# A two-layer decoder with routed experts on one core: the router by halves of the tokens, and the first expert matrix's gather by chunks

## The chip, the cores and the metric

One Trainium2 (trn2) chip, of which one core is used. The metric is the device time of one execution in microseconds; the time before is the median of three executions. All arithmetic is in float32.

## The reference, cut to what matters

Two layers over 256 tokens of width 1024. In each layer a mixer is added to x (retention and a gated linear recurrence in layer 0, stick-breaking and differential attention in layer 1), and then a mixture of experts:

```python
x = x + mix
h = rms_norm(x, norm_ffn[l])
g_logits = h @ wg_r + bg_r                 # 4 groups: the best one is taken
e_logits = h @ we_r + be_r                 # 32 experts, 8 in a group: the best two of the group
gate = p_g * softmax(top_v)                # p_g: the group's softmax probability
a = silu(xb @ w_gate[e]) * (xb @ w_up[e])  # per expert, 1024 -> 512
y = a @ w_down[e]                          # 512 -> 1024, weighted by gate and summed per token
x = x + y
```

rms_norm divides each token's row by the root of its mean square and multiplies by a gain per column. Each expert's three matrices hold 2 MiB each; all 32 experts of both layers are read, 402 MB of the 447 MB that the kernel moves.

## The kernel before

The kernel gives each engine a program of its own, tied by semaphores (`then_inc`, `wait_ge`). Names end in the layer; "half" below means 128 of the 256 tokens (`tc` 0 or 1), which are the partitions of one tile.

**Weights.** SBUF has twelve places of 2 MiB (`places`). The sync engine's program issues every load in a fixed order (lines 436 to 498). Before each it waits until TensorE's count `unit_used` says that the place is free. A unit is one expert's matrix; experts go in quads of four, with twelve units (four of `w_gate`, four of `w_up`, four of `w_down`). When the router begins, the units of quad 0 are loaded or under way; the thirteenth (u = 12) goes into the place of the first. In the gate matrix of quad 0 the four units are stored by quarters of the rows (`QUARTERED`): TensorE frees one after each two chunks of 128 rows. Units 12 to 15 are loaded one by one, those from 16 on four at a time (`load_matrices`, line 391), when all four of a matrix are free. The up matrix of quad 0 is what load 16 waits for.

**The end of the mixer.** `project_out` (line 1109) makes the sums of the output projection. VectorE adds them to x: half 0 whole, half 1 in two parts of 512 columns (lines 1545 to 1551). TensorE transposes x (`turn_x`), and ScalarE copies it into hT and takes the squares (`finish_mixer`, line 1364). The norm's roots are asked for by VectorE (`norm_root`, `inverse_root`), begun by ScalarE with a logarithm and an exponential (`take_root`, line 861), and refined by VectorE with four narrow steps (lines 856 to 859). `ROOTS` lists the requests in order; both engines follow it.

**The router.** TensorE, in this order (`route_and_experts`, line 1140): the strips of half 0 (the router's weights by hT, eight matmuls), a transposition, the first four strips of half 1, the logits of half 0, the other strips of half 1, `start_sums` for accumulator bank 0 (x by the identity, which puts x into the sums of the experts' outputs), the logits of half 1 once ScalarE has copied its strips, `start_sums` for banks 1 to 3, and two filler matmuls (`keep_busy`). VectorE (`route`, line 1582) waits for the logits of both halves, scales them by the roots and adds the bias (line 1602), and finds for each expert by how many of its group it is beaten: differences of all pairs (line 1605), a comparison (1606), a sum (1608), 640 elements wide each; then the group mask (1609) and `picked` (1611). TensorE counts by matmuls with a triangle of ones at which place in its expert each token stands (lines 1170 to 1174), and VectorE keeps it in `rank` (1617).

**The gather.** Each expert has 32 slots in a pass, a quad 128. `one_hots` (line 796) builds `sel`, tokens by slots, by comparing `rank` with 1 to 32 (793), and multiplies it by the roots (799). TensorE multiplies x by it, chunk by chunk of 128 columns, both halves summed in PSUM (line 577); ScalarE writes each chunk to xT with the gain (line 743). For quad 0 TensorE gathers chunks 0 to 3, multiplies chunks 0 and 1 by the gate matrix (line 631), gathers 4 to 7, and goes on. Then, for this and every other quad: up matrix; gather for the next quad; silu(gate) times up by ScalarE and VectorE (lines 760, 820, 823); transpositions (673, 675) of it and of the weighted one-hots `selw`; down matrix; and the outputs are spread back to the tokens (line 565) while the next gate matrix runs. The combine weights are made in `gates` (line 1627) behind the one-hots, with two exponentials on ScalarE (`route`, line 1378) and a load of the sigmoid table behind them. `largest_count` gives the largest number of tokens of an expert; with more than 32, further passes follow (`pe.If(count > SLOTS)`).

## Time and profile before

| | |
|---|---|
| median of three executions | 1168.0 us (1166.81 to 1169.35) |
| the profiled execution's own time | 1166.55 us |
| its span, first to last instruction | 1164.8 us |
| TensorE matmuls busy | 876.4 us (75%) |
| VectorE, ScalarE busy | 223.8 us (19%), 126.7 us (11%) |
| moved by DMA | 447.45 MB, mean 384 GB/s |
| mean granted TensorE clock | 0.877 of full |

The profile is one execution with a record for each instruction. Lines (L631) are lines of the kernel before. An instruction's busy time says what it took, the chain of waits says which work the end of the run hung on, and a table of stretches says what each engine and the DMA engines did between two moments. A float32 matmul appears as two records (x16 is eight matmuls).

### The profile page before, as it was taken

To read this page: it belongs to the slowest core of one execution; us is meant where nothing else is said; L and a number is where in the kernel's file an instruction comes from. 1 tells how busy PE (TensorE), PEld (TensorE's weight loads), DVE (VectorE), ACT (ScalarE), POOL (GpSimd) and SP (SyncE) were. 2 spreads that over 40 slices of the span, in tenths; PEclk is the share of its full clock that TensorE was granted. 3 is DMA by queue.
4 is the path that set the end of the run, shared out by engine and by line. 5 is a ranking of instruction groups with operands and counts; after the bars stand their busy time and mean duration, and the time that the engine had idled before them with its cause. 6 is when DMAs were issued, how large, how long until landed. Compare 5 with 4: busy or idle time off the path is not lost.

```text
span 1164.8 us, 11459 instructions
## 1 busy us (share of the span) xinstructions
PE 876.4 (75%) x5104; PEld 394.0 (34%) x5104; DVE 223.8 (19%) x470; ACT 126.7 (11%) x249; POOL 0.5 (0%) x5
## 2 busy tenths in 40 slices
PE   8999999747474738485899999977474747474776
PEld 7555554212121212121246655433131313131312
DVE  2732332010101010101127541410000101000001
ACT  3411311000000000000021431200000000000000
POOL 0000000000000000000000000000000000000000
PEclk9999999888888877777999999998787878788889
DMA  9776659999999999999996477899999999999997
GB/s 347 304 321 257 267 219 378 430 435 433 435 433 433 435 433 435 435 430 414 424 423 284 154 293 276 317 441 433 433 435 435 433 435 433 433 430 432 417 426 308
DMA packets 19637, 447.45 MB, mean 384 GB/s; under 512 B 2560, under 2 KB 2816, under 8 KB 5504
## 3 DMA queue, kind: packets, MB, share of 16 engines
q1 hardware_dynamic: 19584, 446.67, 91.0%
q8 instruction: 43, 0.70, 0.2%
q14 instruction: 10, 0.08, 0.0%
HBM read 445.61 MB, written 1.05 MB: 383 GB/s over the span
## 4 chain that ended last, share of the span: by engine, by line
DMA 56%; PE 42%; DVE 1%; another core or an unknown queue 1%; issue 0%; ACT 0%; SPq 0%; DVEq 0%
DMA places<-in_together 47%; PE psum L631 14%; PE psum L1016 11%; DMA places<-in_quarters 8%; PE psum L1117 5%; PE psum L1013 4%; PE psum L577 1%; PE psum L1029 1%; PE psum L1057 1%; PE psum L565 1%; DMA places<-in_w_in 0%; PE psum L1144 0%; PE psum L698 0%; PE psum L968 0%
## 5 line engine op out<-in xcount | busy, mean ns | idle before, releaser
L631 PE MATMUL psum<-places,mixed 128*32 128x512 f32 x3040 | 421.8, 707 | 276.3 <-DMA places<-in_together 249.2
L631 PEld LDWEIGHTS psum<-places,mixed 128*32 128x32 f32 x3040 | 110.4, 127 | 570.5 <-issue 448.7
L1016 PE MATMUL psum<-places 128*128 128x512 f32 x288 | 126.3, 593 | 0.0
L1016 PEld LDWEIGHTS psum<-places 128*128 128x128 f32 x288 | 53.6, 190 | 61.4 <-issue 61.2
L577 PEld LDWEIGHTS psum<-sel,x 128*128 128x128 f32 x528 | 60.4, 192 | 17.0 <-issue 15.1
L577 PE MATMUL psum<-sel,x 128*128 128x128 f32 x528 | 64.3, 279 | 1.7 <-DVE sel L799 1.7
L565 PE MATMUL psum<-y_sb,spread 128*128 128x512 f32 x128 | 59.6, 606 | 2.1 <-ACT y_sb L768 1.4
L820 DVE TENSOR_TENSOR sig<-psum,sig 128x512 f32<-128x512 f32 x16 | 11.1, 692 | 253.4 <-ACT sig L760 253.4
L823 DVE TENSOR_TENSOR mixed<-psum,sig 128x512 f32<-128x512 f32 x16 | 11.1, 692 | 245.4 <-PE psum L631 245.4
L833 DVE COPY y_sb<-psum 128x512 f32<-128x512 f32 x14 | 9.7, 692 | 180.2 <-PE psum L631 180.2
L762 ACT COPY mixed<-psum 128x512 f32<-128x512 f32 x16 | 9.4, 586 | 320.6 <-PE psum L675 320.6
L1013 PE MATMUL psum<-places 128*128 128x256 f32 x192 | 42.9, 381 | 0.0
L1013 PEld LDWEIGHTS psum<-places 128*128 128x128 f32 x192 | 36.1, 190 | 5.7 <-issue 1.0
L760 ACT ACTIVATE sig<-psum 128x512 f32<-128x512 f32 x16 | 9.6, 597 | 255.9 <-PE psum L631 255.9
L565 PEld LDWEIGHTS psum<-y_sb,spread 128*128 128x128 f32 x128 | 22.8, 189 | 38.6 <-issue 33.7
L768 ACT COPY y_sb<-psum 128x512 f32<-128x512 f32 x16 | 9.4, 586 | 209.2 <-PE psum L631 181.8
L1117 PE MATMUL psum<-places,y_sb 128*128 128x512 f32 x64 | 28.2, 594 | 0.7 <-ACT small L1396 0.7
L1117 PE MATMUL psum<-places 128*128 128x512 f32 x64 | 28.5, 592 | 0.0
L826 DVE TENSOR_TENSOR mixed<-psum,consts 128x512 f32<-128x512 f32 x32 | 21.9, 690 | 31.8 <-PE psum L577 31.8
L1117 PEld LDWEIGHTS psum<-places,y_sb 128*128 128x128 f32 x64 | 11.9, 190 | 14.8 <-issue 13.9
L1388 ACT ACTIVATE places<-psum,small 128x512 f32<-128x512 f32 x16 | 10.1, 684 | 57.7 <-PE psum L1016 53.6
L1117 PEld LDWEIGHTS psum<-places 128*128 128x128 f32 x64 | 11.8, 190 | 13.4 <-issue 13.4
(252 smaller groups left out, 505.4 us busy)
## 6 DMA issues: line engine op xcount, KB each, us to landing
places<-in_singles SPq DMA_DIRECT2D x32, 2048.0 KB, 10.1
places<-in_quarters SPq DMA_DIRECT2D x22, 2048.0 KB, 35.1
places<-in_w_in SPq DMA_DIRECT2D x12, 2048.0 KB, 26.7
places<-in_w_out SPq DMA_DIRECT2D x4, 2048.0 KB, 14.3
places<-in_quarters SPq DMA_DIRECT2D x4, 1024.0 KB, 45.6
places<-in_w_in SPq DMA_DIRECT2D x2, 1024.0 KB, 27.2
places<-in_w_in SPq DMA_DIRECT2D x3, 512.0 KB, 8.7
x<-in_x SPq DMA_DIRECT2D x2, 512.0 KB, 13.6
```

Source lines behind the costliest of these rows:

```text
L565: mm = pe.matmul(psum[:, ACC + 2 * n + tc, :], spread[:, tc, :], y_sb[:, 512 * n:512 * (n + 1)], start=False, stop=False, skip_group_check ...
L577: mm = pe.matmul(psum[:, YB + c // 4 if bank is None else bank, (c % 4) * P:(c % 4 + 1) * P], x[:, tc, c * P:(c + 1) * P], sel[:, tc, :], ...
L631: mm = pe.matmul(psum[slots, out + n, :], inp[:, c, slots], slot(layer, unit)[:, at + 512 * n:at + 512 * (n + 1)], start=c == 0, stop=c == ...
L820: turn(nc.vector.tensor_tensor(sig, psum[:, GATE, :], sig, ALU.mult))
L823: nc.vector.tensor_tensor(flat(act_h), psum[:, UP, :], sig, ALU.mult).then_inc(m["act_ready"], 1)
L826: nc.vector.tensor_tensor(xT[:, 4 * half:4 * half + 4, :], psum[:, 6 + half, :].rearrange("p (c s) -> p c s", s=P), gain_cols[:, 2 + layer ...
L1013: mm = pe.matmul(banks[:, m // 2, (m % 2) * SEQ:(m % 2 + 1) * SEQ], w[:, c, m * P:(m + 1) * P], hT[:, c, :], start=c == 0, stop=c == KC - 1)
L1016: mm = pe.matmul(banks[:, m, :], hT[:, c, m * P:(m + 1) * P], w[:, c, :], start=c == 0, stop=c == KC - 1)
L1029: mm = pe.matmul(psum[:, 4 + m, 0:SEQ], w[:, c, m * P:(m + 1) * P], hT[:, c, :], start=c == 0, stop=c == KC - 1)
L1057: mm = pe.matmul(banks[:, m, :], hT[:, c, m * P:(m + 1) * P], w[:, c, :], start=c == 0, stop=c == KC - 1)
L1117: return pe.matmul(psum[:, OUT_BANK[layer] + 2 * tc + n, :], mixT(half)[:, c, tc * P:(tc + 1) * P], w[:, c, 512 * n:512 * (n + 1)], start= ...
L1388: r = nc.scalar.activation(dst[:, tc * 512:(tc + 1) * 512], proj(g)[:, tc, :], function, scale=small[:, 2 + tc:3 + tc])
```

## The change

- **Roots by half.** Each layer asks for two roots, one per half. Half 0's is asked for as soon as its square is there, while the output matmuls of half 1 run; half 1's behind the picks of half 0. ScalarE serves the second one ahead of its copy of half 1's strips.
- **Router by half.** Scores, differences, comparison, sum, mask and pick are done for half 0 (320 wide) once its logits are there, then for half 1. Ranks are one matmul for half 0, and two in one sum for half 1. The last addition to x moves from the end of the mixer to the head of `route`, in the same place of VectorE's order. The best expert's mask moves to `gates`.
- **No roots in the one-hots.** `sel` stays 0 or 1. Two matmuls of one column (`scale_slots`) bring the roots of the tokens to their slots, ScalarE keeps them in `slot_scale`, and they enter in the sigmoid's scale and in VectorE's two products.
- **Gather by chunks.** For quad 0, half 0's share of chunks 0 and 1 is gathered when half 0's one-hots are there, then half 1's, then the scale; chunks 2 and 3 are gathered ahead of the third chunk of the gate matrix, 4 and 5 ahead of the fourth, 6 and 7 ahead of the sixth. The exponentials and the table load of ScalarE follow the last of these.
- **TensorE's order.** `start_sums` for bank 0 stands between the ranks of half 0 and of half 1, and for banks 1 to 3 between the gate and the up matrix of quad 0; the counting of the largest number is a pair of matmuls behind the gather of chunks 2 and 3; the count is read ahead of the last quad's branch.

```diff
...
-ROOTS = ((2, 2), (20, 8), (28, 8), (2, 2), (2, 2), (44, 16), (44, 16), (44, 8), (2, 2))
+ROOTS = ((2, 2), (20, 8), (28, 8), (2, 1), (3, 1), (2, 2), (44, 16), (44, 16), (44, 8), (2, 1), (3, 1))
...
+def count_picked(pe):
+    pe.matmul(psum[:, 5, 64:96], ones[:, 0:P], picked[:, 0, :], start=True, stop=False)
+    pe.matmul(psum[:, 5, 64:96], ones[:, 0:P], picked[:, 1, :], start=False, stop=True).then_inc(S["ranks_done"], 1)
...
+    def scale_slots(bank):
+        for tc in range(TC):
+            mm = pe.matmul(psum[:, bank, SEQ:SEQ + 1], sel[:, tc, :], small[:, 2 + tc:3 + tc], start=tc == 0, stop=tc == TC - 1)
...
-    def gather_rest():
-        gather_chunks(4, 8).then_inc(m["gathered"], 1)
-        pe.wait_ge(m["xT_ready"], 1)
+            gather_some(4 * half, 4 * half + chunks, YB + half, range(TC)).then_inc(m["gathered"], 1)
+    def begin_gather():
+        pe.wait_ge(S["sel_first"], layer + 1)
+        gather_some(0, 1, YB + 1, (0,))
+        gather_some(1, 2, YB, (0,))
+        pe.wait_ge(m["sel_ready"], 1)
+        gather_some(0, 1, YB + 1, (1,)).then_inc(S["gather_begun"], 1)
+        gather_some(1, 2, YB, (1,))
+        scale_slots(YB).then_inc(S["gather_begun"], 1)
+    def go_on_gathering(c):
+        begun = 3 * layer
+        if c == 0:
+            pe.wait_ge(S["xT_begun"], begun + 1)
+        elif c == 1:
+            pe.wait_ge(S["xT_begun"], begun + 2)
+        elif c == 2:
+            gather_some(2, 4, YB + 1, range(TC)).then_inc(m["gathered"], 1)
+            count_picked(pe)
+            pe.wait_ge(m["xT_ready"], 1)
+        elif c == 3:
+            gather_some(4, 6, YB, range(TC)).then_inc(S["gather_begun"], 1)
+        elif c == 4:
+            pe.wait_ge(S["xT_begun"], begun + 3)
+        elif c == 5:
+            gather_some(6, 8, YB + 1, range(TC)).then_inc(m["gathered"], 1)
+        elif c == 6:
+            pe.wait_ge(m["xT_ready"], 2)
...
+            matrix(0, 0, GATE, xT, KC, FF, each_chunk=go_on_gathering)
+            start_sums(pe, layer, (1, 2, 3))
+            pe.wait_ge(S["route_ready"], layer + 1)
...
-        mm.then_inc(m["turned"], 1)
+            pe.transpose(psum[:, UP, tc * P:(tc + 1) * P], selw[:, tc, :], ident)
+        scale_slots(UP).then_inc(m["turned"], 1)
...
+    count = pe.value_load(over_i[0:1, layer:layer + 1], min_val=0, max_val=SEQ)
     with pe.If(count > SLOTS):
...
+    def begin_gathered():
+        begun = 3 * layer
+        act.wait_ge(S["gather_begun"], begun + 1)
+        gained_chunks(0, 1, YB + 1, 0).then_inc(S["xT_begun"], 1)
+        act.wait_ge(S["gather_begun"], begun + 2)
+        gained_chunks(1, 2, YB, 0).then_inc(S["xT_begun"], 1)
+        keep_scale(YB)
+        act.wait_ge(m["gathered"], 1)
+        gained_chunks(2, 4, YB + 1, 0).then_inc(m["xT_ready"], 1)
+        act.wait_ge(S["gather_begun"], begun + 3)
+        gained_chunks(4, 6, YB, 0).then_inc(S["xT_begun"], 1)
+        act.wait_ge(m["gathered"], 2)
+        gained_chunks(6, 8, YB + 1, 0).then_inc(m["xT_ready"], 1)
+        gate_exps(layer)
...
-        nc.scalar.activation(sig, psum[:, GATE, :], ACT.Sigmoid).then_inc(m["sig_ready"], 1)
+        nc.scalar.activation(sig, psum[:, GATE, :], ACT.Sigmoid, scale=slot_scale).then_inc(m["sig_ready"], 1)
         act.wait_ge(m["turned"], n16 + i + 1)
         nc.scalar.copy(actT, psum[:, GATE, :].rearrange("p (c s) -> p c s", c=FC))
+        keep_scale(UP)
...
-        placed(sel, quad)
-        nc.vector.tensor_tensor(sel, sel, small[:, 2:4].unsqueeze(2).broadcast_to([P, TC, P]),
-                                ALU.mult).then_inc(m["sel_ready"], 1)
+        placed(sel, quad).then_inc(m["sel_ready"], 1)
...
-        nc.vector.tensor_tensor(flat(act_h), psum[:, UP, :], sig, ALU.mult).then_inc(m["act_ready"], 1)
+        nc.vector.scalar_tensor_tensor(flat(act_h), psum[:, UP, :], slot_scale, sig, ALU.mult, ALU.mult).then_inc(m["act_ready"], 1)
...
+def mean_square(dve, layer, tc):
+    dve.wait_ge(S["squares"], SQUARES[2 * layer] + (1, 3)[tc])
+    return nc.vector.tensor_scalar(small[:, 2 + tc:3 + tc], small[:, tc:tc + 1], 1.0 / D, EPS, ALU.mult, ALU.add)
...
-        logits(0)
+        logits(0).then_inc(S["logits_done"], 1)
         pe.wait_ge(S["xT_third"], layer + 1)
-        strips(1, range(KC // 2, KC)).then_inc(S["strips"], 1)
-        start_sums(pe, layer, (0,))
+        strips(layer, 1, range(KC // 2, KC)).then_inc(S["strips"], 1)
         pe.wait_ge(S["last_strips_kept"], layer + 1)
         logits(1).then_inc(S["logits_done"], 1)
-        start_sums(pe, layer, (1, 2, 3)).then_inc(S["sums_started"], 1)
+        pe.wait_ge(S["picked_ready"], TC * layer + 1)
+        pe.matmul(psum[:, 4, 0:32], before, picked[:, 0, :], start=True, stop=True).then_inc(S["ranks_done"], 1)
+        start_sums(pe, layer, (0,))
+        pe.wait_ge(S["scores_read"], layer + 1)
+        pe.matmul(psum[:, 5, 0:32], ones[:, 0:P], picked[:, 0, :], start=True, stop=False)
         keep_busy(pe, 2, 7, ident, consts[:, 0:SEQ])
-        pe.wait_ge(S["picked_ready"], layer + 1)
-        both = picked.rearrange("p c e -> p (c e)")
-        pe.matmul(psum[:, 5, 0:64], before, both, start=True, stop=False, skip_group_check=True)
-        mm = pe.matmul(psum[:, 5, 32:64], ones[:, 0:P], picked[:, 0, :], start=False, stop=True, skip_group_check=True)
-        mm.then_inc(S["ranks_done"], 1)
-        pe.matmul(psum[:, 4, 0:32], ones[:, 0:P], picked[:, 0, :], start=True, stop=False)
...
+        pe.wait_ge(S["picked_ready"], TC * layer + 2)
+        pe.matmul(psum[:, 5, 0:32], before, picked[:, 1, :], start=False, stop=True).then_inc(S["ranks_done"], 1)
         moe_pe(pe, layer, 0, 0)
...
         keep_xT(layer, 0, slice(0, 2), nc.scalar.copy).then_inc(S["xT_first"], 1)
+        take_root(act, turn)
...
+        ask_root(mean_square(dve, layer, 0), 2, 1)
         dve.wait_ge(S["out_second"], layer + 1)
         V.tensor_tensor(x[:, 1, 0:512], x[:, 1, 0:512], sums(1)[:, 0:512], ALU.add).then_inc(S["added"], 1)
+        refine_root(dve, turn)
...
+        def differences(tc):
+            turn(V.tensor_tensor(by_duel(tc), rows_of(tc).unsqueeze(2).broadcast_to(each),
+                                 rows_of(tc).unsqueeze(3).broadcast_to(each), ALU.subtract))
+        def pick(tc):
+            by_row = pairs(tc).rearrange("p (r n) -> p r n", r=n_rows)
+            turn(V.tensor_tensor(by_row, by_row, const("earlier_wins").unsqueeze(1).broadcast_to([P, n_rows, PER_GROUP ** 2]),
+                                 ALU.is_gt))
+            turn(V.tensor_reduce(beaten_by[:, tc].rearrange("p (r e) -> p r e", e=PER_GROUP), by_duel(tc), AX, ALU.add))
+            turn(V.tensor_scalar(g_hot[:, tc], beaten_by[:, tc, N_EXPERTS:N_EXPERTS + N_GROUPS], 1.0, None, ALU.is_lt))
+            in_group = g_hot[:, tc].unsqueeze(2).broadcast_to([P, N_GROUPS, PER_GROUP])
+            and_wait(dve, V.scalar_tensor_tensor(by_group(picked[:, tc]), by_group(beaten_by[:, tc, 0:N_EXPERTS]), 2.0, in_group,
+                                                 ALU.is_lt, ALU.mult), S["picked_ready"], TC * layer + tc + 1)
+        def place_first(tc):
+            dve.wait_ge(S["ranks_done"], 3 * layer + tc + 1)
+            turn(V.scalar_tensor_tensor(rank[:, tc, 0:32], psum[:, 4 + tc, 0:32], 1.0, picked[:, tc], ALU.add, ALU.mult))
+            return V.tensor_tensor(sel[:, tc].rearrange("p (e s) -> p e s", e=TILE),
+                                   const("iota").unsqueeze(1).broadcast_to([P, TILE, SLOTS]),
+                                   rank[:, tc, 0:TILE].unsqueeze(2).broadcast_to([P, TILE, SLOTS]), ALU.is_equal)
...
+        finish_x(layer)
+        dve.wait_ge(S["strips"], TC * layer + 1)
+        keep_strips(0, V.tensor_copy).then_inc(S["strips_kept"], 1)
+        dve.wait_ge(S["squares"], SQUARES[2 * layer] + 2)
+        scores(0)
+        differences(0)
+        pick(0)
+        dve.wait_ge(S["squares"], SQUARES[2 * layer + 1])
+        turn(V.tensor_tensor(small[:, 1:2], small[:, 1:2], small[:, 7:8], ALU.add))
+        ask_root(mean_square(dve, layer, 1), 3, 1)
+        refine_root(dve, turn)
+        scores(1)
+        V.memset(small[:, 60:61], 0.0).then_inc(S["scores_read"], 1)
+        differences(1)
+        pick(1)
+        place_first(0).then_inc(S["sel_first"], 1)
+        place_first(1).then_inc(M[layer]["sel_ready"], 1)
+    def largest_count(layer):
+        sc = rt[:, 18:19]
+        dve.wait_ge(S["ranks_done"], 3 * layer + 3)
+        turn(V.tensor_reduce(sc[:, 0:1], psum[:, 5, 64:96], AX, ALU.max))
...
+        largest_count(layer)
         dve.wait_ge(S["group_exp"], layer + 1)
...
```

## Rows read from the trace of the kernel before

**Rows 1.** The page, part 4: the chain that ended last, by engine.
```profile
...
DMA 56%; PE 42%; DVE 1%; another core or an unknown queue 1%; issue 0%; ACT 0%; SPq 0%; DVEq 0%
...
```

**Rows 2.** Stretches: PE, PEld, DVE, ACT, POOL busy (instructions), PEclk, DMA share, GB/s.
```profile
...
176.10:179.00 2.90, 2.90 (x26) 1.34 (x25) 1.46 (x9) 2.27 (x6) 0.00 (x0) 1.00 0.04 11
179.00:199.00 20.00, 19.05 (x175) 9.36 (x177) 5.62 (x12) 2.60 (x7) 0.00 (x0) 1.00 0.99 404
199.00:589.00 390.00, 252.19 (x1694) 90.08 (x1686) 35.13 (x63) 14.30 (x28) 0.00 (x0) 0.82 1.00 432
...
741.30:744.00 2.70, 2.70 (x25) 1.14 (x24) 1.34 (x8) 2.23 (x6) 0.00 (x0) 1.00 0.03 6
...
764.00:1154.00 390.00, 252.53 (x1698) 90.25 (x1690) 35.09 (x63) 14.30 (x28) 0.00 (x0) 0.81 1.00 431
...
```

**Rows 3.** Layer 0's chain from strips to second matrix: start, us, what.
```profile
...
166.75 0.34 PE psum L1149 x2
...
167.69 1.06 PE psum L558 x2
...
169.00 0.44 DVE mixed L1602 x2
...
169.46 0.84 DVE mixed L1605
...
172.52 0.43 PE psum L1170 x2
172.95 0.21 PE psum L1171 x2
...
173.25 0.24 DVE rank L1617
...
173.51 0.44 DVE sel L793
...
173.97 0.43 DVE sel L799
...
174.45 2.05 PE psum L577 x16
176.51 1.85 PE psum L631 x16
178.36 1.98 PE psum L577 x16
180.34 12.28 PE psum L631 x112
...
192.63 28.94 DMA places<-in_together
```

**Rows 4.** VectorE (DVE) in order of time, layer 0's router.
```profile
...
165.63 0.29 DVE L979 COPY mixed<-psum 128x128 f32<-128x128 f32 x1 [0.35 <-PE psum L1144]
...
167.16 0.16 DVE L856 TENSOR_TENSOR small<-small 128x2 f32<-128x2 f32 x1 [0.72 <-ACT small L867]
...
167.75 0.16 DVE L859 TENSOR_TENSOR small<-small 128x2 f32<-128x2 f32 x1
...
```

**Rows 5.** ScalarE (ACT) in order of time, layer 0's router.
```profile
...
166.69 0.21 ACT L866 ACTIVATE small<-small 128x2 f32<-128x2 f32 x1
166.92 0.20 ACT L867 ACTIVATE small<-small 128x2 f32<-128x2 f32 x1
...
175.65 0.63 ACT L743 ACTIVATE mixed<-psum,consts 128x128 f32<-128x128 f32 x2 [7.65 <-PE psum L577]
...
```

**Rows 6.** TensorE (PE) in order of time, layer 0's router.
```profile
...
168.72 2.82 PE L558 MATMUL psum<-x,consts 128*128 128x512 f32 x6
171.38 1.03 PE L553 MATMUL psum<-consts 128*128 128x256 f32 x4
...
```

**Rows 7.** Stretches around one wait of TensorE, columns as in rows 2.
```profile
...
543.60:547.40 3.80, 0.01 (x1) 0.01 (x1) 0.27 (x1) 0.00 (x0) 0.00 (x0) 1.00 1.01 431
...
548.30:552.20 3.90, 0.58 (x1) 0.00 (x0) 0.00 (x0) 0.00 (x0) 0.00 (x0) 0.50 1.01 429
...
```

158 lines of the change are left out of this document (68 added, 90 removed).

## The prediction

> **What bounds the kernel.** I read the page first. Transfers hold 56% of the chain that ended last and TensorE 42% [rows 1]. A share says nothing of what a change in one stage is worth, so the next view is a table of stretches [rows 2]. From 199 us to 589 us in layer 0, and from 764 us to 1154 us in layer 1, the DMA engines are busy all the time, at 432 and 431 GB/s. That is the stream of expert weights. No engine's work in these 780 us shortens the run, unless it keeps the stream from its start. Just ahead of it the engines are empty: 11 GB/s from 176.1 to 179.0 us, 6 GB/s from 741.3 to 744.0 us. All twelve places are full, and the next unit (u = 12) may be fetched only when TensorE has used the first quarter of the first gate matrix. So the price of the router is read there: each microsecond by which that quarter is used earlier moves the whole stream, and all behind it, by one, as long as the stream then has no hole. The waits of the router that don't reach this point are worth nothing.
>
> The chain through layer 0's router is next [rows 3]. The logits of the first half end at 166.75 + 0.34 = 167.09 us. VectorE begins with them only at 169.00, when both halves are there. One-hots with the roots multiplied in are ready at 174.40. TensorE gathers four chunks (2.05 us), multiplies the first two (1.85 us), and frees the quarter at 178.36 us. The third transfer of the stream, which fetches a whole matrix, is issued at 192.63, when the up matrix is used. Layer 1 has the same gap 565 us later [rows 2], and I take its chain as a copy of layer 0's.
>
> **What the change does to the quarter.** I rebuild the chain for layer 0, with 0.03 to 0.04 us between two dependent VectorE steps and 0.06 to 0.11 us from one engine to another, as the starts and ends in rows 3 leave between them.
> - VectorE can begin at 167.09 + 0.11 = 167.20, which is 1.8 us earlier. The strips themselves stand where they stood, and the new root of the first half lies ahead of them, while the output matmuls run; it costs nothing, and without this cover it would cost the 1.2 us that the next root is priced at. On ScalarE it moves the first-half square by about 0.4 us, which nothing waits for.
> - Three passes are done by halves, 320 wide in place of 640. A 640-wide pass takes 0.84 us [rows 3], a 256-wide one 0.44: 1.04 ns an element, so 0.50 us for 320 wide, 0.53 with its gap. Between the nearest rows the bounds are half of 0.84 (0.42) and 0.50; I take 0.50, because 256 wide is near. First half: scores 0.25, three passes 1.59, group mask 0.21, pick 0.20, so picked at 169.45.
> - Then the second half's root stands in the middle: an addition and a mean (0.36 with gaps, by the 0.16 us of a narrow step [rows 4]), ScalarE's logarithm and exponential (166.69 to 167.12 us [rows 5], 0.5 with the hand-over), four refining steps (167.16 to 167.91 us [rows 4], 0.75). It ends near 171.15. Behind this wait ScalarE also holds back the copy of the second half's strips, which it does after the root (0.27 us, 170.4 to 170.7), and TensorE the logits behind that, until 171.1: late by 2.4 us, and just hidden by the refining.
> - Second half: scores and marker 0.31, passes 1.59, mask and pick 0.41: picked at 173.46, which is 1.0 us later than now (172.48, where rows 3 has TensorE start at 172.52). Rank (0.24) and a one-hot of half the width (0.30, as 128 wide takes 0.29 [rows 4]) follow for each half: 174.06 and 174.63. The ranks of the second half are one matmul, 0.43 us [rows 3], ready at 174.0, in time. Saved here: the multiplication by the roots, 0.43. So the one-hots are ready at 174.63 in place of 174.40, 0.23 us later.
> - TensorE: a gather matmul takes 2.05/8 = 0.26 us. The two of the first half (0.51) run before 174.63; the two of the second end at 175.20; two matmuls with the roots follow, 0.21 each (the narrow ones of rows 3): 175.62. ScalarE's first chunk (0.63 us for two [rows 5]) is ready at 175.4. Two chunks of gate, 1.85: the quarter is free at 177.47 in place of 178.36.
>
> **Gain per layer: 0.9 us; with both, 1.8 us**, and the rest is whether the stream stays whole. The second quarter: gather 1.03, counting matmuls 0.42, a stall of 0.35 for ScalarE's two chunks, a chunk of 0.88, gather 1.03, a chunk of 0.88: 182.06 us, as now (178.36 + 1.98 + 1.75). A 2 MiB unit at 432 GB/s takes 4.85 us; begun at about 178.1 it ends at 183.0, when the next is just due. I take off 0.1 us a layer. The third transfer: the sums of banks 1 to 3 now stand between gate and up, 2.7 us [rows 6]. From the quarter to the end of up is 3.09 + 0.42 + 0.35 + 12.28 + 2.7 = 18.8 us, so 196.3 in place of 192.63, 3.7 us later. Four units at 432 GB/s last 19.4 us, to about 198.3. From the issue (178.4) to first data was under 1 us, since 20 us at 404 GB/s are 8.1 of the 8.4 MB [rows 2]. So this edit costs nothing, under a cover of 1 us; with that gone, all beyond is paid.
>
> By the Trainium skill, DMA: Bandwidth & Descriptors, section Latency and other measured facts, a first byte comes some 600 ns after the issue; by this the cover would be 1.4 us and the sum the same. It agrees with rows 2 as a bound.
>
> A rule speaks against the halves: VectorE: DVE Perf Modes, section The TRN2 errata, of the Trainium skill says that each instruction pays a fixed time, so that small tiles pay it more often, and gives (N + 151)/0.96 ns; by this 320 wide is 0.49 us and the sum is unchanged. The 0.84 us of the 640-wide row agrees.
>
> In the quads: one 0.43 us VectorE pass fewer, two narrow matmuls and a ScalarE copy of one column more, all under the stream, where TensorE is busy 252 of 390 us [rows 2]. Cover gone, they would cost 0.6 us in each of 16 quads. The count is read by TensorE just ahead of the last quad, also in a wait.
>
> **Sum:** 2 x 0.8 = 1.6 us off the profiled execution's 1166.55 (span 1164.8), so 1164.95. That execution is 1.45 us under the median of 1168.0; on that scale, 1166.4 us, or 0.14% faster. A measurement of this kernel can tell 0.2%, 2.3 us, from no change.
>
> **The rivals.**
> - *More gain* (chance 0.26). If a halved pass takes near half (0.42), three passes of each half save 0.5 us a layer more, and if hand-overs are on the short side, 0.3 more: 2.4 to 3.2 us in all, 1164.8 to 1165.6. For it: picks and masks are also narrower. Against: the fixed part of the narrow rows.
> - *The clock of TensorE* (0.14), the case on the other side. From 167.7 to 170.7 us TensorE now waits for the held-back strips, where it ran sums before (from 167.69 [rows 3]), and until 174.1 has only some 3 us of work. In this trace the clock went to its lower level (0.50, 1.2 GHz) after a wait of 3.8 us (543.6 to 547.4) with little work behind it [rows 7]. The new wait is 3.0. If it falls there, the sum of bank 0 and the filler (1.03 us [rows 6]) take twice as long and the second half's ranks start at 175.5 in place of 173.5: 2.0 us, less the gain, 1.2 us slower a layer; if it stays low through gather and the first chunks, 2.8 more. In all 2.4 to 8 us slower, 1170.4 to 1176. It decides if the wait is long enough to bring the clock down, in both layers. If in one alone, there is no change. The Trainium skill's page TensorE: Matmul & The Clock Gate, section HAM oscillation, has the same rule, that waits make the clock fall and it must be earned again; rows 7 agree.
> - *The gain is eaten* (0.10). The up matrix ends over 1 us later than I have it, or the second quarter does, and the stream has holes of up to 0.8 us a layer: 1166 to 1168.5. The stream is then no longer moved by the router, but by TensorE's work after it.
>
> **Chances.** The forecast has 0.50. Faster by over 0.2%: the first rival and the edge of the forecast, 0.28. Slower by over 0.2%: most of the clock case, 0.13. Within: 0.59. The range goes from 1164.0, the larger gain with the scatter of a median, to 1170.0, the lower end of the clock case.
>
> **What would show it.** Per layer: picked for the second half about 1.0 us later against the strips; a wait of TensorE of 3 us after the strips; the first gate matmul about 0.8 us earlier; the DMA gap shorter by 0.9 us; the third transfer issued 3.7 us later with no gap in DMA ahead of it. I am wrong if the DMA rate dips near 197 to 199 us, if the granted clock falls in the router, or if the stream's 780 us change in length.

## The result, and the profile after

The changed kernel takes 1172.17 us (median of 6 runs, 1170.87 to 1176.85); the kernel before, beside it, 1168.05 us (6 runs). The ratio is 1.0040, 95% interval [1.0030, 1.0051]: 0.4% slower, where 1166.4 us and a small gain were forecast. The profiled execution took 1170.87 us, with a span of 1169.1 us. Its page has 11669 instructions in place of 11459, and part 4 begins:

```profile
DMA 49%; PE 47%; another core or an unknown queue 1%; issue 1%; ACT 1%; DVE 1%; SPq 0%; DVEq 0%
```

Against [rows 1], 7 points have gone from the transfers to TensorE, ScalarE and "issue". The end no longer hangs on the last weights alone.

The stretches of the changed kernel, with the columns of [rows 2]; the last two are those in which the profile has a low clock:

```profile
176.10:179.00 2.90, 2.90 (x26) 1.45 (x26) 0.19 (x1) 0.58 (x3) 0.00 (x0) 1.00 0.06 17
179.00:199.00 20.00, 19.65 (x154) 8.19 (x153) 4.73 (x17) 4.04 (x10) 0.00 (x0) 1.00 0.98 392
199.00:589.00 390.00, 253.31 (x1764) 96.58 (x1762) 35.36 (x60) 16.31 (x38) 0.00 (x0) 0.83 1.00 431
...
173.40:176.80 3.40, 3.40 (x20) 2.95 (x22) 2.43 (x12) 0.55 (x2) 0.00 (x0) 0.61 0.87 371
736.60:743.40 6.80, 6.68 (x25) 5.29 (x25) 4.32 (x20) 0.27 (x2) 0.00 (x0) 0.55 0.84 355
```

The stream still runs at 431 GB/s, and TensorE's load in it is as before. New is the clock (the column after the engines): 0.61 and 0.55 in the two routers, so mostly at the lower level of 1.2 GHz. TensorE in order of time, layer 0's router (start, us, engine, line, in brackets the wait before it):

```profile
170.74 0.41 PE L1176 MATMUL psum<-both_strips,mixed 128*128 128x40 f32 x2 [2.84 <-ACT mixed L1038]
...
171.20 1.10 PE L559 MATMUL psum<-x,consts 128*128 128x512 f32 x2
...
172.29 1.71 PE L554 MATMUL psum<-consts 128*128 128x256 f32 x4
173.78 0.51 PE L1232 MATMUL psum<-picked,consts 128*128 128x32 f32 x2
174.21 2.04 PE L583 MATMUL psum<-sel,x 128*128 128x128 f32 x8
176.07 0.51 PE L590 MATMUL psum<-small,sel 128*128 128x1 f32 x4
176.51 1.92 PE L668 MATMUL psum<-places,mixed 128*32 128x512 f32 x16
```

And layer 1's:

```profile
736.72 0.65 PE L1176 MATMUL psum<-both_strips,mixed 128*128 128x40 f32 x2 [2.84 <-ACT mixed L1038]
...
737.60 2.05 PE L559 MATMUL psum<-x,consts 128*128 128x512 f32 x2
...
739.73 2.05 PE L554 MATMUL psum<-consts 128*128 128x256 f32 x4
741.58 0.47 PE L1232 MATMUL psum<-picked,consts 128*128 128x32 f32 x2
741.86 1.53 PE L583 MATMUL psum<-sel,x 128*128 128x128 f32 x8
...
743.66 1.92 PE L668 MATMUL psum<-places,mixed 128*32 128x512 f32 x16
```

TensorE waits 2.84 us for ScalarE's copy of the strips. In layer 0 the gather then takes 2.04 us for 8 records, twice what the forecast used; in layer 1 the sum of bank 0 takes 2.05 us and the filler 2.05 us for 4 records, against 1.10 us in layer 0 and 1.03 us in [rows 6]. The ranks of the second half are behind them, and VectorE waits for these in layer 1:

```profile
742.09 0.19 DVE L1690 SCALAR_TENSOR_TENSOR rank<-psum,picked 128x32 f32<-128x32 f32 x1 [1.78 <-PE psum L1232]
```

In layer 0 nothing else is late, as VectorE shows (its strips began at 164.70 us, 0.21 us after those of the trace before):

```profile
167.42 0.26 DVE L1657 SCALAR_TENSOR_TENSOR mixed<-psum,small,consts 128x40 f32<-128x40 f32 x1 [1.29 <-PE psum L1176]
167.71 0.49 DVE L1673 TENSOR_TENSOR mixed<-mixed 128x320 f32<-128x320 f32 x1
...
169.49 0.19 DVE L1684 SCALAR_TENSOR_TENSOR picked<-mixed 128x32 f32<-128x32 f32 x1
...
171.14 0.16 DVE L910 TENSOR_TENSOR small<-small 128x1 f32<-128x1 f32 x1
...
173.41 0.19 DVE L1684 SCALAR_TENSOR_TENSOR picked<-mixed 128x32 f32<-128x32 f32 x1
...
174.56 0.29 DVE L1691 TENSOR_TENSOR sel<-consts,rank 128x128 f32<-128x128 f32 x1
```

The last row ends at 174.85, where the forecast, shifted by 0.21, has 174.84. A third place that was not forecast is the last quad of layer 1, in the chain that ended last:

```profile
1129.94 3.63 PE psum L566 x8
1133.85 1.07 PE psum L668 x8
1134.92 4.43 issue
1139.35 7.53 PE psum L668 x56
```

Behind the branch on the count TensorE does four matmuls (8 records) and then stands for 4.43 us without waiting for anything that the profile shows. It never catches up: the last half matrix begins 427.80 us after the layer's first strip, with no wait, where before it began at 424.51 with a wait for its weights.

### The profile page after: what moved, and what is told of

Read it like the earlier page. It is cut to its first block, busy times and chain, and to the rows that moved or that the text cites. A ratio compares the mean times of both kernels' runs of the same rounds, so it can differ in the third digit from the quotient of the medians.

```text
span 1169.1 us, 11669 instructions
## 1 busy us (share of the span) xinstructions
PE 883.4 (76%) x5180; PEld 405.5 (35%) x5180; DVE 222.0 (19%) x478; ACT 130.3 (11%) x271; POOL 0.5 (0%) x5
## 4 chain that ended last, share of the span: by engine, by line
DMA 49%; PE 47%; another core or an unknown queue 1%; issue 1%; ACT 1%; DVE 1%; SPq 0%; DVEq 0%
DMA places<-in_together 41%; PE psum L668 17%; PE psum L1075 11%; PE psum L1187 5%; DMA places<-in_singles 4%; DMA places<-in_quarters 4%; PE psum L1072 4%; PE psum L583 2%; PE psum L566 1%; PE psum L1088 1%; PE psum L1116 1%; PE psum L559 1%; PE psum L554 1%; DMA places<-in_w_in 0%
## 5 line engine op out<-in xcount | busy, mean ns | idle before, releaser
L668 PE MATMUL psum<-places,mixed 128*32 128x512 f32 x3040 | 417.5, 699 | 270.4 <-DMA places<-in_together 242.6
L867 DVE SCALAR_TENSOR_TENSOR sig<-psum,slot_scale,sig 128x512 f32<-128x512 f32 x16 | 12.0, 750 | 245.2 <-ACT sig L810 245.2
L870 DVE SCALAR_TENSOR_TENSOR mixed<-psum,slot_scale,sig 128x512 f32<-128x512 f32 x16 | 12.0, 751 | 240.5 <-PE psum L668 240.5
L810 ACT ACTIVATE sig<-psum,slot_scale 128x512 f32<-128x512 f32 x16 | 11.0, 687 | 242.5 <-PE psum L668 242.5
```

The lines of the kernel that those rows point to most:

```text
L668: mm = pe.matmul(psum[slots, out + n, :], inp[:, c, slots], slot(layer, unit)[:, at + 512 * n:at + 512 * (n + 1)], start=c == 0, stop=c == ...
L867: turn(nc.vector.scalar_tensor_tensor(sig, psum[:, GATE, :], slot_scale, sig, ALU.mult, ALU.mult))
L870: nc.vector.scalar_tensor_tensor(flat(act_h), psum[:, UP, :], slot_scale, sig, ALU.mult, ALU.mult).then_inc(m["act_ready"], 1)
```

## The experiments

One profiled execution of each kernel is compared, from the first strip of a layer on, because the time ahead of it varied by up to 2.7 us between executions whose code is equal up to there (164.5 us before, 167.2 in c5). "Quarter" is the time from the layer's first strip (L1144 of the kernel before, L1171 of the changed one) to the start of the record behind the 16 records of gate matmuls that free the first quarter, in layers 0 and 1. "To the end" runs from layer 0's first strip to the end of the span; the kernel before and its first three variants below, which do the same work, spread by 1.1 us in it. "Tail" says what stands in layer 1's last quad: a gap in front of which the profile puts nothing but issue, or the third quarter of the last matrix begun 6.0 to 6.4 us behind the second in place of 4.8 to 5.0 ("late").

| kernel | median us (runs) | ratio, 95% interval | quarter | to the end | tail |
|---|---|---|---|---|---|
| before | | | 13.80, 13.82 | 1000.3 | clean |
| before, count read late (c5) | 1167.77 (10) | 0.9999 [0.9989, 1.0009] | 13.81, 13.81 | 1001.4 | clean |
| before, 190 empty instructions (d2) | 1167.84 (10) | 0.9996 [0.9987, 1.0006] | 13.80, 13.81 | 1001.4 | clean |
| before, 172 empty instructions (f1) | 1168.23 (11) | 0.9995 [0.9986, 1.0005] | 13.81, 13.82 | 1000.5 | clean |
| before, sums later (e3) | 1173.20 (7) | 1.0031 [1.0018, 1.0044] | 16.11, 15.77 | 1005.4 | clean |
| changed | 1172.17 (6) | 1.0040 [1.0030, 1.0051] | 13.67, 14.84 | 1004.4 | gap 4.43 |
| changed, count early (c1) | 1172.36 (6) | 1.0041 [1.0027, 1.0055] | 14.81, 13.60 | 1004.0 | gap 3.90 |
| changed, 48 empty instructions (d1) | 1173.91 (8) | 1.0047 [1.0030, 1.0065] | 13.63, 14.99 | 1006.3 | gap 4.89 |
| changed, filler in quad 2 (e1) | 1171.99 (7) | 1.0027 [1.0014, 1.0040] | 13.59, 14.83 | 1006.6 | late |
| filler in the wait (c2) | 1169.56 (10) | 1.0012 [1.0002, 1.0022] | 12.81, 12.82 | 1001.5 | late |
| sums in the wait (c3) | 1170.38 (10) | 1.0019 [1.0009, 1.0029] | 12.82, 12.84 | 1003.6 | gap 4.99 |
| c3, 48 empty instructions (d3) | 1169.17 (10) | 1.0008 [0.9999, 1.0018] | 12.82, 12.83 | 1003.3 | gap 4.91 |
| d3, counting matmuls later (d4) | 1171.01 (10) | 1.0025 [1.0015, 1.0035] | 12.81, 12.82 | 1003.4 | gap 4.71 |
| c3, filler in quad 2 (e2) | 1169.46 (11) | 1.0006 [0.9996, 1.0016] | 12.81, 12.83 | 1001.5 | late |
| e2, 50 empty instructions (f2) | 1169.26 (11) | 1.0009 [0.9999, 1.0020] | 12.82, 12.83 | 1001.5 | clean |
| e2, 100 empty instructions (f3) | 1168.36 (11) | 1.0001 [0.9991, 1.0010] | 12.82, 12.84 | 1000.5 | clean |
| f3, gathers behind chunk 3 (g1) | 1167.55 (12) | 0.9998 [0.9989, 1.0007] | 12.81, 12.82 | 999.5 | late |

The kernel before had medians of 1167.89 to 1168.49 us beside them.

### The count, and the wait

**c1**, the count read where it was, behind the first gate matrix:

```
 # TensorE, quad 0
             pe.wait_ge(S["route_ready"], layer + 1)
+            counts.append(pe.value_load(over_i[0:1, layer:layer + 1], min_val=0, max_val=SEQ))
...
-    count = pe.value_load(over_i[0:1, layer:layer + 1], min_val=0, max_val=SEQ)
-    with pe.If(count > SLOTS):
+    with pe.If(counts[0] > SLOTS):
```

> The changed kernel, but TensorE reads the largest count right behind its wait for it, after the gate matrix of quad 0, as the kernel before did in that stage, and no longer just ahead of the last quad's branch. Theory A (the late read holds up TensorE's sequencer at the branch; the profile of the changed kernel has 0.28 and 4.43 us of issue idle there in layer 1, 0.66 in layer 0): the 4.4 us gap is gone, TensorE again waits for the last quarters, and the time falls from about 1172.1 to 1171 or less. Rival (the gap is chance, or belongs to code loading and moves with any edit): the gap stays or turns up elsewhere, the time stays at 1172.

1.0041, with a gap of 3.90 us: the late read is not to blame.

**c5**, the other way round: the kernel before with its count read just ahead of the branch.

> The kernel before, with the read of the count moved to just ahead of the last quad's branch, as in the changed kernel. Theory A: an issue gap of some us appears in TensorE's last quad, and the time rises by 0.5 to 2 us over 1168.0. Rival (the gap comes from the changed kernel's longer code, not from the read): no gap, 1168.0.

0.9999, with gaps of at most 0.79 us. Where the count is read costs nothing in either kernel.

**c2**, the changed kernel with six filler matmuls in the new wait:

```
+    keep_busy(pe, 6, 7, ident, consts[:, 0:SEQ])
     pe.wait_ge(S["last_strips_kept"], layer + 1)
```

> The changed kernel with six filler matmuls (256 columns each, about 2.6 us) behind the last strips, where TensorE waits about 2.8 us for ScalarE's copy. Nothing else moves. Theory B (the wait brings the clock down, and gather and filler at half clock cost the 0.9 us gained per layer): granted clock 1.00 through both routers, the first gate matmul 0.9 to 1.2 us earlier against the strips, the time 1.8 to 2.4 us lower, near 1170. Rival (the stream of transfers has holes behind the first quarter anyway, so the router's clock is not what costs): the clock stays up but the time moves by less than 1 us.

The ratio falls from 1.0040 to 1.0012, and the intervals don't meet. TensorE in layer 0 of this kernel, and its stretches around both routers (clock 1.00):

```profile
168.70 2.86 PE L554 MATMUL psum<-consts 128*128 128x256 f32 x12
171.61 0.42 PE L1176 MATMUL psum<-both_strips,mixed 128*128 128x40 f32 x2
...
175.08 1.17 PE L583 MATMUL psum<-sel,x 128*128 128x128 f32 x8
```
```profile
171.00:179.00 8.00, 7.54 (x50) 4.64 (x49) 4.90 (x22) 1.32 (x6) 0.00 (x0) 1.00 0.78 332
736.00:744.00 8.00, 7.54 (x49) 4.61 (x49) 4.91 (x23) 1.34 (x6) 0.00 (x0) 1.00 0.79 337
```

The fillers do no useful work and take 2.86 us, and by them the gather takes 1.17 us again. The first quarter is free 12.81 us after the strips in both layers: 1.0 us sooner than in the kernel before, and 0.86 and 2.02 us sooner than in the changed one. The fillers also took the gap in the last quad away, so the 2.6 us between the medians aren't the clock's alone.

**c3**, useful work in the same wait:

```
+    start_sums(pe, layer, (0, 1, 2))
     pe.wait_ge(S["last_strips_kept"], layer + 1)
     logits(1).then_inc(S["logits_done"], 1)
...
-    start_sums(pe, layer, (0,))
+    start_sums(pe, layer, (3,))
...
-            start_sums(pe, layer, (1, 2, 3))      # between gate and up
```

> The changed kernel with the accumulators of banks 0 to 2 started in that same wait, bank 3 behind the first half's ranks, and none between the gate and the up matrix of quad 0. Theory B and C together (C: the sums between gate and up delay the third transfer of the stream past the end of the second, a hole of about 1 us per layer): clock 1.00, up matrix used 2.7 us earlier, the time 3 to 4 us lower, near 1168.3. Rival (C is wrong, there was cover enough): the same time as with the filler, near 1170.

The same quarter, and the third transfer is issued 29.5 us after the strips in place of 32.4 (c2). It doesn't help: the last half matrix of layer 0 begins 424.62 us after the strips, in c2 424.46, before 424.53. So the late third transfer cost nothing that can be seen, and c3 is no better than c2 (1170.38 us); it has the gap, c2 has not. As the changed kernel has the gap too, the 1.8 us from 1172.17 to 1170.38 are mostly the clock's.

**e3**, the clock's test in the kernel before: the same wait made there.

```
 # kernel before, behind logits(1)
-    start_sums(pe, layer, (1, 2, 3)).then_inc(S["sums_started"], 1)
-    keep_busy(pe, 2, 7, ident, consts[:, 0:SEQ])
...
 # quad 0, behind the gate matrix
+    start_sums(pe, layer, (1, 2, 3))
```

> The kernel before with its start sums 1 to 3 moved from the router's wait to behind the gate matrix of quad 0 (where the changed kernel has them) and its two router fillers taken out, so that TensorE stands idle for some 3.6 us between the logits and the ranks, in each layer. Clock theory: the granted clock falls to 0.5 for 3.4 to 6.8 us behind that wait as in the changed kernel, the gather of 16 matmuls takes about twice its 2.05 us, the first quarter is freed 1 to 3 us later than 13.80 us after the first strip, and the time is 1 to 5 us longer (1169 to 1173). Rival (the thin matmuls of the new router bring the fall, not the wait): clock 1.00, time within 0.7 us of 1168.

TensorE in layer 0, and its stretches:

```profile
170.09 0.31 PE L1151 MATMUL psum<-both_strips,mixed 128*128 128x40 f32 x2
174.02 0.69 PE L1170 MATMUL psum<-picked,consts 128*128 128x64 f32 x2 [3.63 <-DVE picked L1611]
...
176.39 3.78 PE L577 MATMUL psum<-sel,x 128*128 128x128 f32 x16 [0.45 <-DVE sel L801]
```
```profile
174.00:177.40 3.40, 2.93 (x12) 2.79 (x13) 2.45 (x11) 0.00 (x0) 0.00 (x0) 0.50 1.01 434
...
741.50:745.00 3.50, 3.05 (x13) 2.92 (x14) 2.52 (x12) 0.00 (x0) 0.00 (x0) 0.50 1.00 431
```

The old router, with a wait of 3.63 us and none of the new router's steps in it, is 0.3% slower: the gather takes 3.78 us in place of 2.05 [rows 3], and the quarters come 2.3 and 2.0 us later. So a wait of this length with little work beside it brings the clock down without the new router's narrow matmuls.

### The gap in the last quad

The profile has an instruction queue, whose records are loads of 16 KB of code beside the stream. While TensorE works they come about every 125 matmul records, each of which has a weight load. In the changed kernel two of them start at 1131.3 and 1137.0 us, and the gap ends at 1139.35; in c3 at 1130.0 and 1136.1, and its gap ends at 1138.59. The Trainium skill, page Advanced Engine Details and Errata, section ISA Cache, gives a cache line of 16 KB, or 256 instructions; the size agrees with the records. So the place of the code could decide. Empty instructions in quad 3 of layer 0 were to move it:

```
 # TensorE, quad 3 of layer 0
+    for _ in range(48):          # d2: 190, in the kernel before
+        pe.nop()
```

> The changed kernel with 48 no-operations of TensorE in a covered wait of layer 0 (quad 3), which only shift its later code. Theory D: TensorE's code comes in blocks of 16 KB (the trace's instruction queue), each fetched when the one before is entered, some 5.7 us apart beside the weight stream; in the changed kernel the branch ahead of layer 1's last quad lands some 20 instructions before a block's end, so TensorE stands 4.4 us for the next one. Shifted by 48 the branch lands early in a block: no issue gap in the last quad, TensorE waits for the last quarters again, the time 1 to 2 us lower than the changed kernel, 1170.2 to 1171.2. Rival (the gap is due to the changed order or to the branch itself): gap and time stay, 1172.2.

> The kernel before with 190 such no-operations in the same covered wait. Theory D: this puts its branch ahead of layer 1's last quad near a block's end, and an issue gap of 3 to 5 us appears there though nothing else was changed; as the weights of that quad land late anyway, it costs 0 to 2 us (1168 to 1170). Rival: no gap, 1168.0.

> The variant with the sums of banks 0 to 2 in the new wait, with the 48 no-operations. Its earlier profile had the first quarter of the gate matrix 1.0 us earlier than the kernel before, the stream about 0.5 and 0.8 us ahead, and lost it all, some 4 us, to a 5 us code gap in the last quad. Theory B, C and D together: clock 1.00, no gap, 1166.3 to 1167, faster than the kernel before by about 1.3 us. Rival (something else eats it): 1169 to 1170.

All three missed. The gap stayed in d1 (4.89 us) and d3 (4.91), always behind the same four matmuls, and didn't appear in d2. But the profiles don't show that the edit moved any code. The first lines of four pages, of the kernel before, d2, the changed kernel and d1:

```profile
span 1164.8 us, 11459 instructions
span 1165.8 us, 11459 instructions
span 1169.1 us, 11669 instructions
span 1172.3 us, 11669 instructions
```

No empty instruction is among the records, and the code loads stand at the same matmuls. In layer 1's last quad, counted in matmul records from the layer's first strip, the last three loads begin at 1817, 1854 and 1922 in the kernel before and at 1817, 1854 and 1926 in d2, though 190 instructions are three quarters of a block of 256. The changed kernel has its last five at 1810, 1852, 1864, 1892 and 2002, d1 at 1810, 1852, 1864, 1884 and 1982, where c3, without empty instructions, has the last two as well. Over layer 1's first fourteen loads both pairs agree within a record on average. So d1, d2 and d3 say nothing about the place of the code. If nothing moved, they are repeats of the changed kernel, of the kernel before and of c3, and show how far medians of such repeats lie apart: up to 1.7 us.

**d4** is d3 with the counting matmuls moved from gate chunk 2 to chunk 6.

> As the last one, and the two matmuls that count the largest number moved from ahead of the third chunk of the gate matrix to ahead of the seventh, where TensorE waits for ScalarE. Theory E (the second transfer of the stream starts late, since the second quarter is freed no earlier than in the kernel before, and this costs 0.3 to 0.5 us per layer): the delay of the stream at 4.2 MB falls by 0 to 0.4 us, the time by up to 0.5 us against the last one. Rival: no change, as the wait for ScalarE stands there instead.

1.0025 and a gap of 4.71 us. The second unit was still asked for 17.9 us after the strips, so nothing came earlier, and the fourth unit and the matrix behind it were asked for 0.7 us later than in d3 (23.25 and 30.20 us for 22.57 and 29.51). Its median is 1.8 us above d3's but only 0.6 us above c3's, so whether the edit costs anything isn't settled.

**e1** uses filler matmuls, which the profile does record, in a wait that is covered:

```
 # TensorE, quad 2 of both layers, behind the spreading of the outputs
+    keep_busy(pe, 6, UP, ident, consts[:, 0:SEQ])
```

> The changed kernel with six 128x256 filler matmuls after the gate sums of quad 2 of each layer, where TensorE waits for weights anyway (0.7 us of work, covered). The router is untouched, so the clock must fall there as it did. Theory A (where TensorE's code falls decides whether it loses 4.4 us behind the branch of the last quad; the c2 filler had shifted the code by the same number of matmuls and lost nothing there): the gap with issue in front of it in layer 1's last quad is under 1.5 us, and the time is some 1.5 us below the changed kernel, near 1170.5. Rival B (the gap hangs on the clock or on the router): the gap stays at 4 to 5 us and the time at 1172.

The gap is gone, here and in **e2**, the same edit on c3:

> Start sums of x in the router's wait (the clock stays up, first quarter freed 12.8 us after the first strip) together with the same six fillers in quad 2. Theory A: no issue gap over 1.5 us in layer 1's last quad, and some 1 to 1.5 us less than the 1170.4 that the same kernel took without the fillers, so 1169. Rival B: the gap stays and the time is 1170.4. Under both the 1166.4 of the forecast is not reached, since the second quarter and the third transfer give the first microsecond back.

TensorE in layer 1's last quad, e1:

```profile
1134.93 5.36 PE L668 MATMUL psum<-places,mixed 128*32 128x512 f32 x48 [0.44 <-issue]
...
1151.12 1.92 PE L668 MATMUL psum<-places,mixed 128*32 128x512 f32 x16 [1.27 <-DMA places<-in_quarters]
...
1157.55 3.64 PE L668 MATMUL psum<-places,mixed 128*32 128x512 f32 x16 [3.01 <-DMA places<-in_quarters]
```

Of the twelve kernels with the new router, the six with the gap lack those fillers, and the six without it have six more filler matmuls in each layer, in the router (c2) or in quad 2. Where the fillers run differs, their number doesn't, which speaks for the code's place. The loads differ too. In the six with the gap, two begin at matmul records 1850 to 1853 and 1864 or 1865, the second of them during the gap, and TensorE goes on 1.3 to 1.5 us after the second is in. In the six without it they begin at 1863 to 1865 and 1900, so TensorE had gone on between them. That TensorE waits for this code is thus likely; why twelve more matmuls change it was not settled.

What the gap costs is less clear. With the clock kept up, c3, d3 and d4 need 1003.3 to 1003.6 us to the end, c2, e2, f2 and f3 1000.5 to 1001.5. That is 2.2 us between the means, with one execution each. Between the means of the medians it is 1.0 us (1170.19 and 1169.16), and d3, with the gap, is level with c2, e2 and f2. With the clock down its removal bought nothing that can be told (1172.17 and 1171.99 us). In e1's profiled execution, one of its slower ones (1174.26 us), the last two rows show what stood in the gap's place: the weights' third quarter came late, and the matmuls behind that wait ran at the lower level (3.64 us for 1.92). In c2 the late quarter had the same sequel (3.34 us), in e2 it had not (1.92).

Whether that lateness is the code's too was asked by the next three. One empty-instruction count was to bring it into the kernel before, two to take it out of e2:

> The kernel before with 172 empty instructions on TensorE in quad 3 of layer 0, where it waits for weights; nothing else is changed. With 190 of them the 16 KB code load in layer 1's last quad had begun 418.9 us after that layer's first strip instead of 416.3, and the third quarter of the last matrix was not late. Code theory: fewer of them put the load later still, at 420 to 422, right ahead of that quarter's matmuls; they then start some 1.2 us late, behind a wait of 2.6 us instead of 1.5, and the time is 1 us above the kernel before. Rival (where TensorE's code falls costs nothing): that wait stays at 1.5 us and the time within 0.5 us of the kernel before.

> The kernel with the sums in the router's wait and the fillers in quad 2, whose load began at 421.8 and whose third quarter was 1.2 us late, with 50 empty instructions in quad 3 of layer 0. Code theory: the load comes earlier, at 415 to 419, the third quarter waits 1.5 us, no issue gap over 1.5 us, the kernel ends 434.7 us after layer 1's first strip instead of 435.9, and the time is 1168.3, level with or just below the kernel before. Rival: the wait of 2.6 us stays and the time is 1169.5.

> As the run before it with 100 empty instructions instead of 50. Code theory: the load comes earlier again, 408 to 415, no late quarter, time 1168.3. Rival: 1169.5 and the wait of 2.6 us.

f1 missed: the load stayed where it was, and the kernel was unchanged (0.9995). f2 and f3 have no late quarter, but their code loads began at 421.3 and 420.7 us after the strips, and e2's, with the late quarter, at 420.8. So a load at that point doesn't make the quarter late by itself. The page of e2, f2 and f3 has 11717 instructions each, and their loads stand at the same matmuls, so here too the empty instructions aren't shown to have moved the code. If they did nothing, the late quarter comes and goes between executions of one program. What makes it late stays open. f3 is level with the kernel before.

### Where the lead goes

With the clock up and a clean tail the new router frees the first quarter 1.0 us earlier in each layer, and f3 is still not faster. The sync engine's issue of the second unit, in layer 0, first of the kernel before, then of f3 (strips at 164.49 and 166.18):

```profile
182.26 0.33 SPq L369 DMA_DIRECT2D places<-in_singles  x1
```
```profile
184.08 0.33 SPq L370 DMA_DIRECT2D places<-in_singles  x1
```

That is 17.77 us after the strips before, and 17.90 in f3: a gather stands between gate chunks 2 and 3. The first unit had been asked for 1.0 us earlier, so the DMA engines run short: in f3, 20 to 22 us after the strips (186.18 to 188.18), at 344 GB/s, where the kernel before has 451. The rows are those of the kernel before and of f3:

```profile
184.49:186.49 2.00, 2.00 (x24) 0.65 (x20) 0.17 (x1) 0.60 (x1) 0.00 (x0) 1.00 1.05 451
```
```profile
186.18:188.18 2.00, 2.00 (x24) 0.61 (x20) 1.15 (x8) 1.92 (x5) 0.00 (x0) 1.00 0.92 344
```

**g1** is f3 with those gathers moved:

```
 # go_on_gathering(c)
-    elif c == 3:
-        gather_some(4, 6, YB, range(TC)).then_inc(S["gather_begun"], 1)
     elif c == 4:
+        gather_some(4, 6, YB, range(TC)).then_inc(S["gather_begun"], 1)
+        gather_some(6, 8, YB + 1, range(TC)).then_inc(m["gathered"], 1)
         pe.wait_ge(S["xT_begun"], begun + 3)
-    elif c == 5:
-        gather_some(6, 8, YB + 1, range(TC)).then_inc(m["gathered"], 1)
```

> The run before it with 100 empty instructions, and the last two gathers of quad 0 moved from between gate chunks 2, 3, 4 and 5 to behind chunk 3, so that the second quarter is freed without a gather inside it. In all kernels with the new router and the clock up the second unit was asked for 17.90 us after the layer's first strip (before: 17.77), although the first was asked for 1.0 us earlier, and the DMA rate fell to 230 to 360 GB/s for two half-microseconds at 20 to 21 us. If this hole is what eats the lead: the second unit is asked for at 16.8, the third at some 20.8, the hole at 20 us is gone, the last half matmul of layer 0 starts 0.4 us earlier against the strips (before and now 424.3 to 425.1), and the time is 0.4 to 1 us less, 1167.4 to 1168, under the kernel before. Rival (the stream is held back elsewhere, or does not keep a lead at all): the second unit is asked for earlier but the last half matmuls and the time stay, 1168.4.

Its issue, the same stretch, and the last half matrix of layer 0 (strips at 164.35):

```profile
181.02 0.33 SPq L370 DMA_DIRECT2D places<-in_singles  x1
```
```profile
184.35:186.35 2.00, 2.00 (x27) 0.54 (x20) 1.76 (x10) 0.74 (x1) 0.00 (x0) 1.00 0.97 418
```
```profile
587.80 1.06 PE L734 MATMUL psum<-places,mixed 128*32 128x512 f32 x8 [0.56 <-DMA places<-in_quarters]
```

The second unit is asked for at 16.67 us, the rate nearly holds (418 GB/s), and the last half matrix begins 423.45 us after the strips, against 424.53 before and 424.33 in f3. Of the other kernels with the new router and the clock up, one profiled execution each, none is below that (424.33 to 425.24), so g1's lies well outside their spread. The whole microsecond is now kept through layer 0. In layer 1 the third quarter is late again (2.90 us of waiting), and that eats it: 424.85 against 424.51 before. The median is 1167.55 us beside 1168.22 for the kernel before, ratio 0.9998 [0.9989, 1.0007], which can't be told from no change. It is the lowest median of the changed versions, and no version was shown to beat the kernel before.

## Why the prediction was wrong

**The chain of VectorE and ScalarE was right.** Starts and ends against the strips came as worked out: scores at 167.21 (forecast 167.20), first half picked at 169.47 (169.45), root done at 171.09 (171.15), second half picked at 173.39 (173.46), last one-hot 174.64 (174.63), all less the 0.21 us. The 320-wide pass took 0.49 us for 0.50. With the clock up the quarter was free 0.99 us sooner than in the kernel before, for 0.89 forecast.

**The step that failed first** is the line "two chunks of gate, 1.85: the quarter is free at 177.47", because the gather ahead of it was priced at 0.26 us a matmul, a row taken at the upper clock. The text had named the wait (3.0 us; it was 2.84) and the fall as a rival, and gave it 0.14, since the only fall in the rows stood behind 3.8 us. In layer 1 a second step fell with it, the ranks of the second half "ready at 174.0, in time": behind the slow sum and filler they began 10.9 us after the strips, where that rival had put them (175.5, or 11.0), and VectorE waited 1.78 us. The rival came true in both layers: c2 took it away (quarter 0.86 and 2.02 us earlier, time 2.6 us less) and e3 made it in the kernel before. Its price, 2.4 to 8 us above the kernel before, holds the 4.1 us measured, though not all of these are the clock's. Its mechanism was right and the chance too small. "If in one alone, there is no change" wasn't tested. The rule of the Trainium skill named there (TensorE: Matmul & The Clock Gate, HAM oscillation), that waits make the clock fall, agrees with the rows behind the 2.84 us.

**The second step that failed** is "I take off 0.1 us a layer" for the second quarter. The forecast freed it at 182.06, 17.57 us after the strips; the request in f3 comes at 17.90, against 17.77 before. A 0.1 us loss was booked, but most or all of the lead of 1.0 us went. The cover was worked out as if a unit moved at 432 GB/s from its start ("begun at about 178.1 it ends at 183.0"). In the trace before, the first unit is asked for at 178.42 us, and three of the next stretches are:

```profile
178.49:179.49 1.00, 1.00 (x10) 1.00 (x10) 0.93 (x5) 0.17 (x1) 0.00 (x0) 1.00 0.63 131
179.49:180.49 1.00, 1.00 (x12) 0.82 (x14) 0.73 (x2) 0.11 (x1) 0.00 (x0) 1.00 0.94 180
180.49:181.49 1.00, 1.00 (x12) 0.26 (x8) 0.85 (x2) 1.00 (x4) 0.00 (x0) 1.00 0.61 246
```

So the full rate comes only some 3 us behind the request. Data within 1 us, which the text read from rows 2, isn't the full rate: 20 us at 404 GB/s in place of 432 are 1.3 us short. The outcome is that of the rival "the gain is eaten", but its condition, a second quarter over 1 us late, wasn't met: less the 0.17 us from freeing to request, f3's came at 17.73, 0.16 us late. This and the clock came together, and each was priced alone.

**The third transfer** came 33.3 us after the strips in layer 0, where 31.8 was forecast: 0.86 us of that is the clock, the rest mis-sized. It cost nothing that can be seen all the same, since c2 (32.4) and c3 (29.5) reach the last half matrix within 0.2 us of each other. Its cover was summed wrongly: four units of 19.4 us from 178.1 end at 197.5, not 198.3.

**The late count read** cost nothing by itself, as said (c1, c5), and under the stream, at 431 GB/s as before, the quads' added work shows no cost. But the gap of 4 to 5 us behind the branch was in no part of the forecast. It cost at most 1 to 2 us with the clock up, and nothing that can be told in the changed kernel.

**The sum:** of the 4.1 us lost, 1.8 to 2.6 are the clock: 1172.17 to 1170.38 by c3, both with the gap; 1171.99 to 1169.46 from e1 to e2, both with the late quarter; and 1172.17 to 1169.56 by c2, which also has no gap. What is left between 1169.5 and the forecast's 1166.4 is the lead that was given back at the second unit and the tail of layer 1, whose late quarter is measured but not explained. Without the clock's fall the forecast would still have been 2 us or more too low: the lowest median with the clock up and the forecast's order of gathers is f3's 1168.36.

## What to carry to other kernels

When an edit takes work out of a wait on TensorE, ask what clock the work behind it will run at: here 2.84 us of idleness with thin work behind it doubled the price of a gather on the path, and 2.9 us of filler, or as well the next useful matmuls, gave it back. When a transfer is asked for earlier, follow the next requests too: a lead lasts only if the second one comes earlier as well, so rebuild the chain to the second and third release and not only to the first. And where a kernel is bound by a stream to its end, leave some slack in the last stage, because there a delay has no cover. And when an edit is meant to move code, look in the profile for whether it did, before reading its time.

## What the runs showed of the hardware

- The page lists an instruction queue among those of the 16 DMA engines: blocks of 16 KB, 1.0 to 1.1 us each, 43 in the kernel before and 45 in the changed one. Beside a full stream two loads behind the branch of layer 1 start 5.7 to 6.0 us apart, and TensorE stood still for 3.9 to 5.0 us in six kernels until 1.3 to 1.5 us after the second was in (c3: in at 1137.1, resumed 1138.59). Twelve filler matmuls more in the program removed it; why was not settled.
- Empty instructions left no trace: as many instruction records with 48 to 190 of them as without (11459, 11669, 11717), and the code loads at the same matmuls. Whether the program on the chip has them is not known.
- A 2 MiB load asked for with the DMA engines empty runs at 131, 180 and 246 GB/s in the first three microseconds and at 459 in the fourth (kernel before, from 178.49 us).
- The clock fell behind a wait of 2.84 us in both layers of the changed kernel. How much of the work behind it was hit varied between executions of nearly the same code: 13.67 and 14.84 us for the quarters of the two layers in one kernel, 14.81 and 13.60 in c1.
